# Last stage of a two-block network on one core: its output products in two groups of four token tiles instead of 4 + 2 + 2, and another order of banks, buffers and steps where the stage begins

## The chip, the cores and the metric

One core of a Trainium2 chip runs the whole program. The metric is device time in microseconds (us), median of the runs shown. Engines are named as the profile names them: PE (TensorE matmuls), PEld (its weight loads), DVE (VectorE), ACT (ScalarE), POOL (GpSimd), SP (SyncE, which issues nearly all DMAs here; "SPq" is its queue).

## The reference, cut to what matters

A first block (gated delta rule, gated linear attention, convolutional FFN) and a second block (dilated windows, a bidirectional recurrence, cross attention) come before the part that changes. Everything is fp32, 1024 tokens, width 1024. The part that changes is the end of the second block:

```python
h = h + memory_cross_attention(h, mem)  # ends in o @ wo         ("w_co")
hid = square(relu(rmsnorm(h, norm_mlp_g) @ w_mlp_in))       # 1024 -> 4096  ("mlp_in")
h = h + hid @ w_mlp_out                                     # 4096 -> 1024  ("mlp_out")
return rmsnorm(h, norm_final_g)                             # ("norm_final")
```

## The kernel before, in words

**Order.** `schedule` (line 351) writes one list of units. Each engine's program runs through the whole list in that order and does its own share of each unit, so an engine's queue is in order: a wait of one unit holds all that is behind it. SP is such a queue too: it carries panel loads (line 3519), stores of hidden tiles (line 3694), the spill of the residual (line 3682) and the final stores (line 3709).

**Products.** An fp32 factor is split into a high and a low word (fp32r), and a product is three matmuls of 128x512 (`wide`, line 1366). A panel is 512 KB of weights (or of hidden values), [128, 1024] in SBUF. SP loads it, ACT writes its high word (`halve`, line 2778), then POOL (line 3280) or, for panels in `on_dve`, DVE (line 1837) writes the low word over the panel itself. SP loads ahead through a ring of 6 panel slots (10 in the output products); high words sit in a ring of 9. ACT works up to 5 split panels ahead of the unit that uses one, DVE up to 3 of its own, POOL up to 2 of its own. A slot or a high place is free again once PE has done with the last unit that used it.

**Head of the MLP.** `grouped_products` (line 202) does w_co for token tiles (0-3), (4,5), (6,7). Between its units stand the RMS norm of the finished tiles (ACT squares, line 2879; DVE Newton steps, lines 1948 to 1954; ACT xhat, line 2888) and transposes into features: PE line 1363 into a bank, two ACT writes (2864 feat_x, 2865 ftm_hi), one DVE write (2045 ftm_lo) that frees the bank. Steps f1, f2, f3 are the features of the tiles (0-3), (4,5), (6,7); each is 8 chunks of 128 features.

The hidden layer has 16 pairs m of chunks of 128 features, by two halves l of 512 tokens. Pair 0 is computed plainly: `whole(i, l)` is chunk i, half l, 24 matmuls. Pairs 1 to 15 use a seven-product (Winograd) form, `mlp_pair(m)`, products P1, P2, P5, P6, P7, P3, P4 of 12 matmuls each. That form needs sums of weight panels (POOL line 3476, S1 to S4, their high words by ACT line 3215, their low words by POOL line 3454) and sums T1 to T4 of the features (`feature_sums`: DVE lines 2660 to 2663, high words ACT line 3235, low words DVE line 2666). The order at the head (lines 794 to 804) is: `in_split_rest(0)`, which writes `in_first` and `in_b`, the high words of pair 0's second panel (ACT lines 3205, 3206); `whole(0,0)` and `whole(1,0)` in banks 4 and 5; f3, in banks 2, 3, 6, 7, 0, 1 in turn; `in_split(1)`, which writes the sums and words of pair 1's weights; `feature_sums`; `whole(0,1)` and `whole(1,1)` in banks 2 and 3; `in_split_sums(1)`, the words of the weight sums.

ACT copies each whole result out of its bank (`mlp_in`, line 3220) and DVE squares it (line 2670) at the place of its `whole` unit. `in_first` lies in a buffer that w_co uses till its end, so ACT waits there for the last product of w_co (line 3203).

**Output products.** `mlp_out` (line 1799) goes over the groups (0-3), (4,5), (6,7) of tiles (`GROUPS`, line 198). In a group it goes over k0, 16 steps of two chunks each, and in a step over the two halves h of the output width. It holds 8, 4 and 4 banks (`out_banks`, line 832). Each step needs two weight panels, and a panel of hidden values, which for the first group holds two chunks and for the others four; so a group takes 48, 40 and 40 panels, and a step is 48 matmuls in the first group and 24 in the others. When a group ends, DVE adds its banks to the residual (line 2720), then come squares, Newton steps, and further on the `final` steps: DVE line 2071 scales tile n, SP stores it (line 3709) after a wait for that. Tiles 0 to 3 have their `final` at the steps k0 = 14, 16, 18, 20 of the second group, tiles 4 and 5 at k0 = 14 and 16 of the third, tiles 6 and 7 at the end.

Of the kernel before, what the change touches and what calls it, by code (L numbers as in the profile page):

```python
# [350 lines left out]
def schedule(k):  # L351
# [417 lines left out]
    f3, a3 = feats("norm_mlp", (6, 7), (2, 3, 6, 7, 0, 1)), applies("norm_mlp", (6, 7))  # L769
# [32 lines left out]
    for i in range(2):  # L802
        whole(i, 1)
    k.unit("in_split_sums", 1)
    outs = []
    for m in range(1, NPAIRS):
# [19 lines left out]
        for what in PRODUCTS:  # L826
            k.banks.take(("mlp_in", m, what), (4, 5, 6, 7, 0, 1, 2, 3))
# [4 lines left out]
    out_banks = ((5, 6, 7, 0, 1, 2, 3, 4), (5, 6, 7, 0), (1, 2, 3, 4))  # L832

    def final(n):
        return lambda: k.unit("final", n, 0)

    between = {(0, 8): [lambda: k.unit("resid_again")],
               (0, NFF2 - 2): [lambda: norm_start(k, "norm_final", (0, 1, 2, 3))],
               (1, NFF2 - 2): [lambda: norm_start(k, "norm_final", (4, 5))],
               (2, NFF2 - 2): [lambda: norm_start(k, "norm_final", (6, 7)), final(6), final(7)],  # L840
               **{(1, 14 + 2 * n): [final(n)] for n in range(4)}, **{(2, 6 + 2 * n): [final(n)] for n in (4, 5)}}
    for group, tiles, k0, ph, pw in outs:
        for h in range(HALVES):
            if k0 == 0:
                for n in tiles:
                    k.banks.take(("mlp_out", h, n), out_banks[group])
            k.unit("mlp_out", h, k0, tiles, pw[h], ph, used=pw[h],
                   last=("mlp_out", h, tiles[-1]) if k0 == NFF2 - 2 else None)
# [38 lines left out]
def memory(k, nc, stack):  # L887
# [187 lines left out]
    k.in_first = place("in_first", [P, BANK], F32R, at=at(10))  # L1075
# [2689 lines left out]
```

## Time and profile before

| what | value |
|---|---|
| median of 3 runs (lowest, highest) | 2972.49 us (2966.23, 2973.3) |
| the profiled execution's own time | 2970.01 us |
| its span | 2968.8 us, so 1.2 us lie around the span |
| matmul busy share of the span | 95% |
| w_co | from 2207.9 us |
| pair 0 and the features of tiles 6, 7 | 2262.9 to 2302.1 us |
| output products | 2591.5 to 2959.2 us |

The profiled execution lies 2.5 us under the median. A row of a timeline or of the chain of waits gives start, duration, engine, line and operation; in square brackets is the idle time of the engine ahead of it and what ended that. Durations of matmuls overlap, so the pace is read from one start to the next. In a table of stretches the columns are start:end, length, then for each engine the busy time and (xcount) of instructions, then the granted TensorE clock (1.00 is 2.4 GHz, 0.50 is 1.2 GHz), the DMA share and GB/s.

### The profile page before, as it was taken

To read this page: it belongs to the slowest core of one execution; us is meant where nothing else is said; L and a number is where in the kernel's file an instruction comes from. 1 tells how busy PE (TensorE), PEld (TensorE's weight loads), DVE (VectorE), ACT (ScalarE), POOL (GpSimd) and SP (SyncE) were. 2 spreads that over 40 slices of the span, in tenths; PEclk is the share of its full clock that TensorE was granted. 3 is DMA by queue.
4 is the path that set the end of the run, shared out by engine and by line. 5 is a ranking of instruction groups with operands and counts; after the bars stand their busy time and mean duration, and the time that the engine had idled before them with its cause. 6 is when DMAs were issued, how large, how long until landed. Compare 5 with 4: busy or idle time off the path is not lost.

```text
span 2968.8 us, 33195 instructions
## 1 busy us (share of the span) xinstructions
PE 2821.9 (95%) x13188; PEld 2199.7 (74%) x13188; DVE 1658.4 (56%) x2418; ACT 1032.1 (35%) x1577; POOL 989.5 (33%) x565
## 2 busy tenths in 40 slices
PE   6999999999999999999998999999988999999988
PEld 3777567776467888888886678887756888888876
DVE  7556655543874554556556656776345644533454
ACT  2346522223022222222225640674456322132443
POOL 2432012222144444444440214210012877522343
PEclk9999999999999999999999999999998999999999
DMA  7210022214332111111113122113212333364565
GB/s 257 88 41 22 5 82 72 65 57 143 125 94 72 49 50 50 50 49 44 50 43 125 39 57 81 34 42 107 66 42 92 110 110 112 111 227 147 201 235 181
DMA packets 241306, 269.11 MB, mean 91 GB/s; under 512 B 18792, under 2 KB 158464, under 8 KB 241152
## 3 DMA queue, kind: packets, MB, share of 16 engines
q1 hardware_dynamic: 239520, 262.59, 26.9%
q10 hardware_dynamic: 1631, 4.40, 0.4%
q8 instruction: 105, 1.72, 0.2%
q14 instruction: 50, 0.40, 0.0%
HBM read 229.96 MB, written 34.87 MB: 89 GB/s over the span
## 4 chain that ended last, share of the span: by engine, by line
PE 75%; DVE 11%; ACT 6%; DMA 3%; issue 3%; POOL 2%; SPq 0%; ACTq 0%; DVEq 0%; POOLq 0%
PE bank L1370 60%; PE bank L1716 2%; DMA panel<-in_w_mlp_out 2%; PE bank L1518 1%; PE bank L1477 1%; PE bank L1532 1%; PE bank L1700 1%; PE bank L1668 1%; DVE ffn_conv L2403 1%; PE bank L1483 1%; PE bank L1363 1%; DVE ffn_conv L2399 1%; PE bank L1687 1%; DVE mixed L2109 1%; DVE panel_lo L1837 1%
## 5 line engine op out<-in xcount | busy, mean ns | idle before, releaser
L1370 PE MATMUL bank<-ft_hi,panel_lo 128*128 128x512 f32 x1312 | 467.6, 391 | 1.7 <-DVE ftx_lo L2045 1.7
L1370 PEld LDWEIGHTS bank<-ft_hi,panel_lo 128*128 128x128 f32 x1312 | 247.2, 188 | 54.1 <-issue 2.8
L1370 PE MATMUL bank<-ft_hi,panel_hi 128*128 128x512 f32 x704 | 273.9, 389 | 0.0
L1370 PE MATMUL bank<-ft_lo,panel_hi 128*128 128x512 f32 x704 | 273.9, 389 | 0.0
L2399 DVE TENSOR_SCALAR ffn_conv<-ffn_in,ffn_taps 128x512 f32<-128x512 f32 x88 | 114.1, 1297 | 278.8 <-ACT ffn_in L3065 278.6
L3280 POOL TENSOR_TENSOR panel_lo<-panel,panel_hi 128x1024 fp32r<-128x1024 f32 x66 | 158.0, 2401 | 244.3 <-ACT panel_hi L2778 231.1
L1370 PE MATMUL bank<-panelm_hi,panelm_hi 128*128 128x512 f32 x512 | 201.3, 393 | 14.2 <-POOL panel_out_lo L3280 8.6
L1370 PE MATMUL bank<-ft,panel 128*128 128x512 f32 x416 | 202.5, 607 | 2.3 <-ACT sq_inv L3018 0.9
L2403 DVE SCALAR_TENSOR_TENSOR ffn_conv<-ffn_in,ffn_taps,ffn_conv 128x512 f32<-128x512 f32 x176 | 154.5, 878 | 6.2
L1837 DVE TENSOR_TENSOR panel_lo<-panel,panelm_hi 128x1024 fp32r<-128x1024 f32 x52 | 83.5, 1611 | 125.7 <-ACT panelm_hi L2778 125.7
L1370 PEld LDWEIGHTS bank<-ft_hi,panel_hi 128*128 128x128 f32 x704 | 132.1, 188 | 27.5
L1370 PEld LDWEIGHTS bank<-ft_lo,panel_hi 128*128 128x128 f32 x704 | 132.1, 188 | 27.4
L3374 POOL TENSOR_TENSOR ltm_vnew<-lt,masks 128x512 f32<-128x512 f32 x48 | 65.0, 1362 | 249.4 <-PE bank L1518 145.7
L1370 PE MATMUL bank<-panel_hi,ffn_hid_hi 128*128 128x512 f32 x352 | 138.4, 393 | 5.1 <-ACT ffn_in L3065 4.2
L2682 DVE TENSOR_TENSOR mlp_y<-mlp_y,bank 128x512 f32<-128x512 f32 x105 | 72.1, 686 | 125.6 <-ACT mlp_y L3228 74.7
L1370 PE MATMUL bank<-panel_hi,ffn_hid_lo 128*128 128x512 f32 x352 | 138.1, 392 | 0.0
L1370 PE MATMUL bank<-panel_lo,ffn_hid_hi 128*128 128x512 f32 x352 | 138.1, 392 | 0.0
L2778 ACT ACTIVATE panelm_hi<-panel 128x1024 fp32r<-128x1024 f32 x78 | 82.4, 1060 | 148.6 <-DMA panel<-in_w_mlp_out 75.9
L2414 DVE TENSOR_TENSOR resid<-resid,bank 128x512 f32<-128x512 f32 x176 | 111.7, 683 | 35.4 <-PE bank L1370 35.1
L1370 PE MATMUL bank<-panel_lo,panelm_hi 128*128 128x512 f32 x320 | 124.5, 389 | 0.0
L1370 PEld LDWEIGHTS bank<-panelm_hi,panelm_hi 128*128 128x128 f32 x512 | 96.9, 189 | 37.1 <-POOL panel_out_lo L3280 9.4
L2778 ACT ACTIVATE panel_hi<-panel 128x1024 fp32r<-128x1024 f32 x66 | 69.4, 1054 | 140.6 <-PE bank L1370 102.9
(544 smaller groups left out, 6832.4 us busy)
## 6 DMA issues: line engine op xcount, KB each, us to landing
panel<-in_w_mlp_out SPq DMA_DIRECT2D x60, 512.0 KB, 6.7
panel<-in_w_in SPq DMA_DIRECT2D x52, 512.0 KB, 3.8
panel<-in_w_ada SPq DMA_DIRECT2D x48, 512.0 KB, 4.1
panel<-in_ffn_w_up SPq DMA_DIRECT2D x44, 512.0 KB, 3.7
panel_out<-in_w_mlp_out SPq DMA_DIRECT2D x36, 512.0 KB, 6.1
panel<-in_w_mlp_in SPq DMA_DIRECT2D x32, 512.0 KB, 5.1
hid<-mlp_y SPq DMA_DIRECT2D x60, 256.0 KB, 2.0
panel<-in_w_o SPq DMA_DIRECT2D x24, 512.0 KB, 3.5
```

What stands on the lines that cost most here:

```text
L1363: m = te.transpose(ps[:, tile(i)], src[:, tile(j)], k.ident[:])
L1370: m = te.matmul(ps, a, b, start=(start and j == 0), stop=(stop and j == len(pairs) - 1))
L1477: m = te.matmul(ps[:, tile(h)], lhs(h), rhs_of(h), start=True, stop=True)
L1716: m = te.matmul(ps[:, at:at + HD + 1], k.p_t[(2 * t + hb) % 4][:, 2 * side + c, :], v, start=(hb == side == c == 0), stop=(hb == side == c ...
L1837: dve.tensor_tensor(lo, k.view(p), hi.bitcast(F32), ALU.subtract).then_inc(*v.new("lowered", p))
L2399: dve.tensor_scalar(out, pre[:, 1 + h * BANK:1 + (h + 1) * BANK], w[:, 0:1], w[:, 3:4], ALU.mult, ALU.add).then_inc(*v.new("ffn_tap", c, g ...
L2403: dve.scalar_tensor_tensor(out, pre[:, 1 + j + h * BANK:1 + j + (h + 1) * BANK], w[:, j:j + 1], out, ALU.mult, ALU.add).then_inc(*v.new("f ...
L2414: evict(dve.tensor_tensor(r, r, v.bank("down", i, h, n)[:], ALU.add), "down", i, h, n)
L2682: return dve.tensor_tensor(out[:], x[:], v.bank("mlp_in", m, what)[:], ALU.add)
L2778: act.activation(k.halves_of(p)[0], k.view(p), ACT.Copy).then_inc(*a.new("halved_hi", p))
L3280: pool.tensor_tensor(lo, k.view(p), hi.bitcast(F32), ALU.subtract).then_inc(*g.new("halved_lo", p))
L3374: pool.tensor_tensor(t.ltm[:], t.lt[:], spread(k.masks[:, lv, :], 1, H4), ALU.mult).then_inc(*g.new("delta_pool", n, "ltm", lv))
```

## The change

1. **Output products**: groups (0-3), (4-7). Every step has a hidden panel of two chunks and two weight panels: 48 + 48 panels. Both groups hold all eight banks, in the order 5, 0, 1, 2, 3, 6, 7, 4.
2. **Between them**: squares of tiles 0 to 3 at k0 = 2, 4, 6, 8 of the second group, Newton steps at 10, finals at 12, 14, 16, 18.
3. **Last chunks**: the steps k0 = 28 and 30 of the second group are done by pairs of tiles: `mlp_last` for (4,5), h = 0 and 1, then norm and finals of 4 and 5; then the same for (6,7).
4. **Head, order**: all of `in_split(0)` stands where its first half stood (after w_co's unit (1,3)). `in_first` has another place, so ACT doesn't wait there for w_co. Both buffer sets of `in_s`, `sums` and `sums_lo` change places between odd and even pairs, so POOL's sums of pair 1 wait for the last w_co product only, no longer for the features and squares of tiles 6 and 7.
5. **Head, banks**: `whole(0,0)`, `whole(1,0)` in banks 6, 7; f3 over banks 0 to 5; the ring of the seven products begins 4, 5, 0, 1, 2, 3, 6, 7.
6. **Feature sums in two halves** of the token columns: those of tiles (0,1) with (4,5) ahead of f3, the rest behind it. High and low words as before, after the second half.
7. **`squared_whole`**: the four copies, squares and stores of pair 0 come together after the last `whole`.

```diff
-    f3, a3 = feats("norm_mlp", (6, 7), (2, 3, 6, 7, 0, 1)), applies("norm_mlp", (6, 7))
+    f3, a3 = feats("norm_mlp", (6, 7), (0, 1, 2, 3, 4, 5)), applies("norm_mlp", (6, 7))
     def whole(i, l):
-        k.banks.take(("mlp_in", 0, i, l), (((4, 5), (2, 3))[l][i],))
+        k.banks.take(("mlp_in", 0, i, l), (((6, 7), (2, 3))[l][i],))
-    k.unit("in_split_rest", 0)
+    in_panels(1)
     for i in range(2):
         whole(i, 0)
+    k.unit("feature_sums", 0)
     for step in f3:
         step()
-    in_panels(1)
     k.unit("in_split", 1)
-    k.unit("feature_sums")
+    k.unit("feature_sums", 1)
     for i in range(2):
         whole(i, 1)
+    k.unit("squared_whole")
     k.unit("in_split_sums", 1)
...
-            for group, tiles in enumerate(GROUPS):
+            for group, tiles in enumerate(((0, 1, 2, 3), (4, 5, 6, 7))):
                 for k0 in range(0, NFF2, 2):
-                    if group == 0 or k0 % 4 == 0:
-                        chunks = 4 if group else 2
-                        ph = k.panel("mlp_hid", (group, k0),
-                                     rows_of(d["hid"], k0 * P, chunks * P, tiles[0] * P, len(tiles) * P), True)
-                        k.hid_key[ph] = min(group, 1), k0 // 2, chunks // 2
+                    ph = k.panel("mlp_hid", (group, k0), rows_of(d["hid"], k0 * P, 2 * P, group * BANK, BANK), True)
+                    k.hid_key[ph] = k0 // 2, group
...
-    out_banks = ((5, 6, 7, 0, 1, 2, 3, 4), (5, 6, 7, 0), (1, 2, 3, 4))
+    out_banks = (5, 0, 1, 2, 3, 6, 7, 4)
     between = {(0, 8): [lambda: k.unit("resid_again")],
-               (0, NFF2 - 2): [lambda: norm_start(k, "norm_final", (0, 1, 2, 3))],
-               (1, NFF2 - 2): [lambda: norm_start(k, "norm_final", (4, 5))],
-               (2, NFF2 - 2): [lambda: norm_start(k, "norm_final", (6, 7)), final(6), final(7)],
-               **{(1, 14 + 2 * n): [final(n)] for n in range(4)}, **{(2, 6 + 2 * n): [final(n)] for n in (4, 5)}}
+               (1, 10): [lambda: k.unit("deviation", "norm_final", 0, 4)],
+               **{(1, 2 + 2 * n): [lambda n=n: k.unit("squares", "norm_final", n)] for n in range(4)},
+               **{(1, 12 + 2 * n): [lambda n=n: k.unit("final", n, 0)] for n in range(4)}}
...
+            if group == 0 or k0 < NFF2 - 4:
+                k.unit("mlp_out", h, k0, tiles, pw[h], ph, used=pw[h],
+                       last=("mlp_out", h, tiles[-1]) if k0 == NFF2 - 2 else None)
...
+    for tiles in ((4, 5), (6, 7)):
+        for h in range(HALVES):
+            k.unit("mlp_last", h, tiles, outs[-2:], used=outs[-1][4][1])
+        norm_start(k, "norm_final", tiles)
+        for n in tiles:
+            k.unit("final", n, 0)
...
-    k.in_first = place("in_first", [P, BANK], F32R, at=at(10))
+    k.in_first = place("in_first", [P, BANK], F32R, at=at(29, 256))
-    k.mlp_first = [place(f"mlp_first{n}", [P, BANK], at=at(8, 2048 * n)) for n in range(4)]
+    k.mlp_first = [place(f"mlp_first{n}", [P, BANK], at=at(26, 2304 + 2048 * n)) for n in range(4)]
...
+    def mlp_last(h, tiles, outs):
+        for n in tiles:
+            ps = pe.bank("mlp_out", h, n)
+            for _, _, k0, ph, pw in outs:
+                w, x = panel(pw[h]), panel(ph)
+                for j in range(2):
+                    m = wide(ps[:], [y[:, j, tile(n - 4)] for y in x], [y[:, j, :] for y in w], False, k0 + j == NFF2 - 1)
+            fill(m, "mlp_out", h, n)
...
-    def feature_sums():
+    def feature_sums(part):
+        cols = slice(2 * P * part, 2 * P * part + 2 * P)
+        (x0, z0), (x1, z1) = ((k.feat_x[l][:, 0:4, cols], k.feat_x[l][:, 4:KD, cols]) for l in range(2))
+        v.wait_ge("ft_hi", "norm_mlp", 4 + 2 * part, KD - 1)
...
     def in_split(m):
             if m == 1:
-                g.wait_ge(*g.filled("feat", "norm_mlp", 6, KD - 1))
-                g.wait_ge("squares", "norm_mlp", NT - 1)
+                for n in (6, 7):
+                    g.wait_ge(*g.filled("w_co", 1, n))
```

## Rows read from the trace of the kernel before

**Rows 1.** The page, busy time of each engine with share and count.

```profile
PE 2821.9 (95%) x13188; PEld 2199.7 (74%) x13188; DVE 1658.4 (56%) x2418; ACT 1032.1 (35%) x1577; POOL 989.5 (33%) x565
```

**Rows 2.** Stretches: head of the MLP; first group of output products; second and third.

```profile
2262.00:2310.00 48.00, 37.35 (x138) 29.30 (x139) 29.13 (x31) 26.40 (x41) 20.63 (x10) 0.82 0.13 44
...
2604.00:2762.00 158.00, 157.82 (x696) 130.70 (x697) 54.28 (x33) 49.05 (x47) 39.29 (x17) 1.00 0.49 179
...
2780.00:2867.00 87.00, 79.10 (x339) 64.31 (x338) 45.84 (x30) 37.37 (x37) 36.82 (x14) 0.98 0.68 235
2867.00:2959.00 92.00, 87.80 (x380) 71.69 (x378) 42.56 (x39) 39.45 (x39) 35.24 (x14) 0.98 0.61 211
```

**Rows 3.** Timeline of PE at the head: last transposes of f2 up to P5.

```profile
2259.41 1.03 PE L1363 MATMUL bank<-ident,xhat 128*128 128x128 f32 x8
...
2262.85 0.67 PE L1370 MATMUL bank<-ftm_hi,in_a 128*128 128x512 f32 x1 [2.41 <-DVE ftm_lo L2045]
...
2273.85 0.79 PE L1370 MATMUL bank<-ftm_hi,in_first 128*128 128x512 f32 x1 [3.67 <-POOL panel_lo L3454]
...
2282.32 1.47 PE L1363 MATMUL bank<-ident,xhat 128*128 128x128 f32 x12
...
2288.87 0.80 PE L1370 MATMUL bank<-ftm_hi,in_a 128*128 128x512 f32 x1 [3.20 <-DVE ftm_lo L2045]
...
2309.64 0.47 PE L1370 MATMUL bank<-feat_x_hi,in_s 128*128 128x512 f32 x1 [1.92 <-POOL sums_lo L3454]
```

**Rows 4.** Timeline of PE in the output products, the first and the longest of seven gaps.

```profile
2604.18 0.50 PE L1370 MATMUL bank<-panelm_hi,panelm_hi 128*128 128x512 f32 x1 [1.61 <-POOL panel_lo L3280]
...
2839.55 0.60 PE L1370 MATMUL bank<-panelm_hi,panelm_hi 128*128 128x512 f32 x1 [5.01 <-POOL panel_out_lo L3280]
```

**Rows 5.** Timeline of SP's queue: a load, and the next final store.

```profile
2829.91 0.78 SPq L3519 DMA_DIRECT2D panel_out<-in_w_mlp_out  x1
...
2843.91 0.36 SPq L3709 DMA_DIRECT2D out<-resid  x1
```

**Rows 6.** Chain of waits, from a panel's load to its low word.

```profile
2844.86 6.25 DMA panel<-in_w_mlp_out
2851.14 1.07 ACT panelm_hi L2778
2852.27 2.36 POOL panel_lo L3280
```

**Rows 7.** Timeline of ACT at the head.

```profile
2267.56 2.19 ACT L2888 ACTIVATE xhat<-resid,rstd 128x1024 f32<-128x1024 f32 x2 [2.41 <-DVE rstd L1954]
...
2270.17 0.61 ACT L3206 ACTIVATE in_b<-panel 128x512 fp32r<-128x512 f32 x1
...
2283.00 0.48 ACT L2864 ACTIVATE feat_x<-bank,cols 128x256 f32<-128x256 f32 x1
...
2288.36 0.59 ACT L2865 ACTIVATE ftm_hi<-bank,cols 128x256 fp32r<-128x256 f32 x1
...
2299.47 5.53 ACT L3235 ACTIVATE feat_x_hi<-feat_x 128x2048 fp32r<-128x2048 f32 x3 [5.70 <-DVE feat_x L2662]
2304.90 1.06 ACT L3220 COPY mlp_first<-bank 128x512 f32<-128x512 f32 x2
2305.83 2.03 ACT L3215 ACTIVATE in_s<-sums 128x1024 fp32r<-128x1024 f32 x2
```

**Rows 8.** Timeline of DVE at the head: feature sums and their low words.

```profile
2289.46 2.28 DVE L2660 TENSOR_TENSOR feat_x<-feat_x,feat_x 128x2048 f32<-128x2048 f32 x1
...
2295.06 4.37 DVE L2662 TENSOR_TENSOR feat_x<-feat_x,feat_x 128x2048 f32<-128x2048 f32 x1
...
2302.78 13.24 DVE L2666 TENSOR_TENSOR feat_x_lo<-feat_x,feat_x_hi 128x2048 fp32r<-128x2048 f32 x4
```

**Rows 9.** Timeline of POOL at the head.

```profile
2306.99 6.87 POOL L3454 TENSOR_TENSOR sums_lo<-sums,in_s 128x1024 fp32r<-128x1024 f32 x2 [6.40 <-ACT in_s L3215]
```

**Rows 10.** Timeline of DVE after the last matmul.

```profile
2959.22 0.69 DVE L2720 TENSOR_TENSOR resid<-resid,bank 128x512 f32<-128x512 f32 x1 [0.67 <-PE bank L1370]
```

More of the change, by code:

```diff
@@ L826, in schedule @@
         for what in PRODUCTS:
-            k.banks.take(("mlp_in", m, what), (4, 5, 6, 7, 0, 1, 2, 3))
+            k.banks.take(("mlp_in", m, what), (4, 5, 0, 1, 2, 3, 6, 7))
         pa, pb = k.in_panels[m]
@@ L845, in schedule @@
                 for n in tiles:
-                    k.banks.take(("mlp_out", h, n), out_banks[group])
-            k.unit("mlp_out", h, k0, tiles, pw[h], ph, used=pw[h],
-                   last=("mlp_out", h, tiles[-1]) if k0 == NFF2 - 2 else None)
+                    k.banks.take(("mlp_out", h, n), out_banks)
+            if group == 0 or k0 < NFF2 - 4:
+                k.unit("mlp_out", h, k0, tiles, pw[h], ph, used=pw[h],
+                       last=("mlp_out", h, tiles[-1]) if k0 == NFF2 - 2 else None)
         k.hid_with[ph], k.last_use[ph] = pw[1], len(k.order) - 1
@@ L2713, in mlp_out, with mlp_last, sums_out @@
     def mlp_out(h, k0, tiles, pw, ph):
-        if k0 != NFF2 - 2:
-            return
+        if k0 == NFF2 - 2:
+            sums_out(h, tiles)
+    def mlp_last(h, tiles, outs):
+        sums_out(h, tiles)
+    def sums_out(h, tiles):
         v.wait_ge("resid_loaded", "again")
@@ L2751, in halve @@
         elif k.panel_list[p][0] in ("mlp_hid", "mlp_out"):
[L2752 removed]
+            a.wait_ge(*a.filled("mlp_in", NPAIRS - (2 if k.high_at[p] in [f"True {n}" for n in range(4)] else 1), "P4"))
         if k.panel_list[p][3] is not None:
@@ L3202, in in_split_rest @@
         if m == 0:
-            for n in (6, 7):
-                a.wait_ge(*a.filled("w_co", 1, n))
             act.activation(k.in_first[:], b[:, 0:BANK], ACT.Copy)
@@ L3208, in in_split_sums @@
     def in_split_sums(m):
-        s = m % 2
-        if m == 2:
+        s = 1 - m % 2
+        if m == 1:
+            for n in (6, 7):
+                a.wait_ge(*a.filled("w_co", 1, n))
+        elif m == 2:
             for n in range(4):
@@ L3216, in in_split_sums, with squared_whole @@
                 *a.new("halved_hi", "S", m, 12 + 22 * n))
-    def mlp_in(i, l):
-        a.wait_ge(*a.filled("mlp_in", 0, i, l))
-        evict(act.copy(k.mlp_first[2 * i + l][:], a.bank("mlp_in", 0, i, l)[:]), "mlp_in", 0, i, l)
+    def squared_whole():
+        for l in range(2):
+            for i in range(2):
+                a.wait_ge(*a.filled("mlp_in", 0, i, l))
+                evict(act.copy(k.mlp_first[2 * i + l][:], a.bank("mlp_in", 0, i, l)[:]), "mlp_in", 0, i, l)
     def mlp_pair(m):
@@ L3228, in mlp_pair, with feature_sums @@
         evict(act.copy(k.mlp_y[n][:], a.bank("mlp_in", m, "P1")[:]), "mlp_in", m, "P1")
-    def feature_sums():
+    def feature_sums(part):
+        if part == 0:
+            return
         a.wait_ge("resid_moved0", "mlp", 0)
@@ L3469, in in_split @@
                 g.wait_ge("panel_loaded%d" % k.slot[p], p)
-            x = [k.sums[s][n // 2][:, n % 2, :] for n in range(4)]
+            x = [k.sums[1 - s][n // 2][:, n % 2, :] for n in range(4)]
             for n, (u, w, op) in enumerate(((b[:, 0:BANK], b[:, BANK:D], ALU.add), (x[0], a[:, 0:BANK], ALU.subtract),
@@ L3513, in load @@
         if p in k.hid_key:
-            l, first, count = k.hid_key[p]
-            for m in range(first, first + count):
-                for i in range(2):
-                    sp.wait_ge("moved%d" % (4 * (m % 2) + 2 * i + l), "hid", m)
+            m, l = k.hid_key[p]
+            for i in range(2):
+                sp.wait_ge("moved%d" % (4 * (m % 2) + 2 * i + l), "hid", m)
         name = "panel_loaded%d" % k.slot[p]
@@ L3694, in store, with squared_whole @@
         sync.dma_start(d["hid"][tile(2 * m + i), half(l)], y[:]).then_inc(*sp.new("moved%d" % n, "hid", m, step=16))
-    def mlp_in(i, l):
-        sp.wait_ge("mlp_square", 0, i, l)
-        store(0, i, l, k.mlp_first[2 * i + l])
+    def squared_whole():
+        for l in range(2):
+            for i in range(2):
+                sp.wait_ge("mlp_square", 0, i, l)
+                store(0, i, l, k.mlp_first[2 * i + l])
     def mlp_pair(m):
```

58 lines of the change are left out of this document (27 added, 31 removed).

## Prediction, written before the change was run

> **What bounds the kernel now.** I read the page first: PE is busy for 95% of the span [rows 1], so only its gaps and its slow stretches can be won. The change adds and removes no matmul. Then the table of stretches, and in the stretches that lose time the timeline of PE with the idle time ahead of each matmul.
>
> The pace to compare with comes from the first group of output products: 696 matmuls in 158 us, 0.227 us each, no gap [rows 2]. So 24 matmuls (a `whole`, or half a step) take 5.45 us, a step of 48 takes 10.9, and one of the seven products takes 2.7. Two places fall short of it.
>
> *Head of the MLP.* From 2262 to 2310 the granted clock averages 0.82 [rows 2]. As the clock has two levels, 1.2 and 2.4 GHz, (1 - 0.82) x 48 = 8.6 us of full-speed work are lost. The gaps are 2.41, 3.67, 3.20 and 1.92 us [rows 3], and the timeline shows the matmuls right behind them at half pace. Each has its own releaser: a bank that a feature write had not freed, the low word of pair 0's second panel, the features of tiles 6 and 7, the low word of the weight sums.
>
> *Second and third group of output products.* 339 matmuls take 87 us where 77.0 would do, and 380 take 92 where 86.3 would do [rows 2]: 10.0 + 5.7 = 15.7 us lost. The longest gap, 5.01 us, ends with POOL's low word of a panel [rows 4]. What made it late stands in SP's queue: load at 2829.91, next final store only at 2843.91 [rows 5]. SP waits for `final`, DVE's `final` stands behind a low word, that behind a load: 14 us a round, against 5.45 us that PE needs for a step of two tiles.
>
> **The change, part by part** (against the profiled execution, 2970.0 us, span 2968.8).
>
> *1. Start of `whole(0,0)`.* Banks 6 and 7 were freed long before (w_co, h = 0), so the wait for a feature write goes. The transposes ended at 2259.41 + 1.03 = 2260.4 [rows 3]. But ACT now writes `in_first` and `in_b`, 0.61 us each [rows 7], ahead of the last features of f1 and f2, and PE's transposes follow ACT there: between 0 and 1.2 us later, and I take 1.0 as ACT has little idle time there. Start 2261.4 instead of 2262.85: gain 1.4.
>
> *2. The two wholes.* The low words of pair 0 are now ready about 2256, as POOL has only their ACT words to wait for, so the 3.67 us gap goes, and with both gaps the slow matmuls. They took 2262.85 to 2282.32, 19.5 us [rows 3]; 48 x 0.227 = 10.9: gain 8.6. Call their end t0: 2272.3 instead of 2282.3. POOL's sums of pair 1 move to 2261, where nothing needs it. xhat of tiles 6, 7 began at 2267.56 and took 2.19 [rows 7]; one microsecond later it still ends (2270.8) before t0.
>
> *3. f3 and `whole(0,1)`.* Before: 6.55 us from t0 to 2288.87 [rows 3]. Now no copy stands ahead of the features on ACT. ACT writes sixteen pieces from 2283.00 to 2288.95 [rows 7], 0.72 us a chunk with its start to start; DVE adds half a microsecond (2288.95 to 2289.46 [rows 7, 8]). The half sums put ahead on DVE are four operations of half of 2.28 us [rows 8], with overhead 1.2 each: from 2268.5 (after the Newton steps) to 2273.4, t0 + 1.1, so they hold the bank writes hardly at all. Chunks 6 and 7 wait for banks 0 and 1, `whole(0,1)` for bank 2 (chunk 2): 0.3 + 3 x 0.72 + 0.5 = 3.0, start at t0 + 3.2. Its last features are there at t0 + 6.6, wanted at 8.0. Gain 3.3.
>
> *4. Up to P5 of pair 1.* PE would come to P5 at t0 + 3.2 + 10.9 + 5.45 = 19.6. What it needs: DVE's second half sums start at t0 + 6.7. Four operations of half length: 2.28 us alone, 4.37 beside POOL for a whole one [rows 8], so 4 x 1.2 = 4.8 to 4 x 2.2 = 8.8; POOL has but two instructions to collide there, so I take 6.6. The third is done at 11.7, then ACT's three high words 5.53, four copies 2.1 (1.06 for two), one weight word 1.0 [rows 7], POOL's low word 2.7 (start 2306.99, PE 2309.64 [rows 9, 3]): 23.1. The four copies, which had been spread, now stand two more in this chain. So PE waits 3.5 us, more than before, yet P5 is at t0 + 23.1 instead of 27.3. Beyond point 3 that is 0.9 of gain; the longer wait costs clock, 0.5, so 0.4. The low words on DVE (13.24 for four [rows 8]) end at t0 + 26.5, before P4 at 34, and the squares behind them end before the stores are wanted. The pairs after that run as now.
>
> The Trainium skill (SBUF - State Buffer, Who interferes with whom) says that a DVE operation with two SBUF inputs and a GpSimd one that reads SBUF lock each other out for the whole instruction. The two durations of the sums agree. Taken for all four sums it would make the 6.6 a full 8.8 and take 2.2 us from the gain.
>
> *5. Start and change of group.* The 1.61 us gap behind the first step [rows 4] stays: the fifth panel still waits for the last pair. At the change of group DVE adds the four banks of h = 0 (0.69 each [rows 10]) while PE does h = 1, and the squares that stood there are spread behind. No cost, one part of a microsecond of gain that I don't count.
>
> *6. Second group.* A step has 10.9 us for three panels, as the first group had, which ran without gap. Loads per 48 matmuls fall from five to three. SP's finals at k0 = 12 to 18: a round of 14 us against 10.9, four times, is 12 us of lag at most, and ten slots are 3.3 steps, 36 us. So 15.7 us come back.
>
> *7. Last pairs of tiles.* `mlp_last` needs the panels of k0 = 30 only 1.4 us after step 26. The latest, the first weight panel, can be loaded when step 24 ends: 6.25 + 1.07 + 2.36 + 0.4 to issue = 10.1 us [rows 6], against 10.9 + 1.4 = 12.3. Bound: with a load of twice that length it would be 4 us late. Norm and finals of tiles 4, 5 run under the last 10.9 us of PE.
>
> *8. Tail.* From the last bank add at 2959.22 [rows 10] to the end, 9.6 us, the steps are the same: 0.
>
> Sum: 1.4 + 8.6 + 3.3 + 0.4 + 15.7 = 29.4 us. The execution becomes 2940.6; it lay 2.5 below the median, so the median is forecast at **2943**. Bounds: the head between 8 (point 4 with 8.8, dips behind the bank waits of f3, more delay in point 1) and 18 (no wait at P5), the output between 10 and 17. Both ends give 2937 to 2954.
>
> **The rivals.**
>
> *A. The head gives back half.* ACT carries the chain of point 4 in order, and PE, early, waits at P5. If copies, sums and lock each come late, P5 stays at t0 + 27.3 as it was and the longer gap (7.7 us) costs 2 us of clock. For it: this wait exists already (1.92 us). Against: half the sums are out of the chain. 29.4 - 4 - 2 = 23: 2949.
>
> *B. Banks.* Both groups hold all eight banks. If DVE's adds queue behind a low word whose panel is late, the second group can't begin: 8 x 0.69 = 5.5 us: 2948. Against: the first change of group in the trace shows only a small gap. The Trainium skill (Perfetto Trace Analysis, Matmuls) asks that groups rotate through different banks, so that one is emptied under the next; by it this wait would come here.
>
> *C. The finals still empty the ring.* If SP's rounds are not covered by the ten slots, 4 x (14 - 10.9) = 12.4 us of gap return: 2955.
>
> *D. The change doesn't do what it says:* the gaps only move, to other panels and other words; gain under 9: about 2970.
>
> *E. Slower.* In the second group every step from k0 = 2 to 26 loses what the longest gap shows, 5.0 us, since hidden panel, weights, squares and finals share SP's and DVE's queues: 13 x 5.0 = 65, so 2972 - 14 - 16 + 65 = 3007. It decides when a round takes longer than the 36 us of the ring; the longest round seen is 14.
>
> **How the numbers follow.** Forecast 0.66, A 0.12, B 0.06, C 0.08, D 0.05, E 0.03. A measurement of this kernel tells about 0.3% (9 us) from no change. Faster by more: forecast, A, B, C, 0.92; within: D, 0.05; slower: E, 0.03. The range runs from 2936 to 2954: the forecast's bounds, A and B.
>
> **What would show it.** In the changed kernel's timeline of PE: no gap before `whole(0,0)` and `whole(1,0)`; they take about 11 us together; short gaps in f3; a gap of 3 to 4 us before P5 ended by `sums_lo`; P1 of the last pair some 14 us earlier. In the output products the gap behind the first step and no other over 1 us, clock 1.00, SP's final stores without long waits. Wrong would be: `whole(0,0)` waiting for POOL, P5 over 25 us behind t0, gaps ended by `panel_lo` in the second group or at `mlp_last`, or a longer tail.

## The result, and the profile after

The changed kernel took 2943.66 us (median of 4 executions, 2942.52 to 2945.87) where the kernel before took 2969.36 (median of 4, 2965.34 to 2973.3) on the same chip: ratio 0.9914, 95% interval 0.9897 to 0.9932. On a second chip, beside the experiments below, it was 2938.75 against 2970.38: ratio 0.9894, 0.9881 to 0.9908. The forecast was 2943, with a range of 2936 to 2954. The profiled execution took 2943.77 us (span 2942.5), 26.3 us less than the profiled one of before.

Two executions of one kernel can't be laid on each other by their absolute times: they differ by some microseconds ahead of the part that was changed. The last common point is the first `w_co` product. This is it in the timeline of PE, in the kernel before, with the wait ahead of the last features of the first group:

```profile
2207.92 0.47 PE L1370 MATMUL bank<-panel_co,mix_co_hi 128*128 128x512 f32 x1 [1.57 <-DVE mix_co_lo L2648]
...
2250.60 0.66 PE L1363 MATMUL bank<-ident,xhat 128*128 128x128 f32 x4 [1.19 <-DVE ftm_lo L2045]
```

And this is the timeline of PE after, from the same point to P5 of pair 1 (the first product that needs the weight sums), with its first gap in the output products:

```profile
2208.63 0.47 PE L1371 MATMUL bank<-panel_co,mix_co_hi 128*128 128x512 f32 x1 [1.57 <-DVE mix_co_lo L2657]
...
2252.13 0.66 PE L1364 MATMUL bank<-ident,xhat 128*128 128x128 f32 x4 [2.06 <-DVE ftm_lo L2054]
...
2254.39 0.63 PE L1371 MATMUL bank<-panel_co,mix_co_lo 128*128 128x512 f32 x1
...
2262.52 0.47 PE L1371 MATMUL bank<-ftm_hi,in_a 128*128 128x512 f32 x1
...
2273.50 0.49 PE L1364 MATMUL bank<-ident,xhat 128*128 128x128 f32 x3
...
2276.86 0.50 PE L1371 MATMUL bank<-ftm_hi,in_a 128*128 128x512 f32 x1 [0.28 <-DVE ftm_lo L2054]
...
2299.70 0.77 PE L1371 MATMUL bank<-feat_x_hi,in_s 128*128 128x512 f32 x1 [6.21 <-POOL sums_lo L3472]
...
2595.39 0.50 PE L1371 MATMUL bank<-panelm_hi,panelm_hi 128*128 128x512 f32 x1 [1.81 <-POOL panel_lo L3298]
```

Against [rows 3] the 2.41 and 3.67 us gaps are gone and the two wholes run through in 10.98 us. The 3.20 is 0.28. But the wait for the low word of the weight sums has grown from 1.92 to 6.21, and a gap of 2.06 us stands ahead of the last features of the first group, where the kernel before has 1.19.

The stretches of the output products (window, its length, PE's busy time and matmuls, granted clock, DMA share, GB/s), against [rows 2]:

```profile
2595.00:2753.00 158.00, 157.61 (x695) 1.00 0.49 179
...
2771.00:2858.00 87.00, 87.00 (x385) 1.00 0.47 163
2858.00:2932.00 74.00, 74.00 (x328) 1.00 0.33 121
```

The second group now has 385 matmuls in 87 us where 339 stood, with no gap; so has the stretch of the change of group and of the last pairs of tiles.

From the first product of `w_co` to the end the times are 2968.8 - 2207.92 = 760.9 and 2942.5 - 2208.63 = 733.9 us: **27.0 us** gained, and 0.7 of it hidden by a later start in this execution. A second profiled execution of the changed kernel gives 733.9 again, though its absolute times lie 0.6 us lower. All single runs below are compared by this time. It doesn't repeat that well for every kernel: the kernel of before with only its last steps changed reaches P5 1.5 us earlier than the kernel before (see its run below), since fewer matmuls run slowly in its head. So a difference of 1 to 2 us between single profiles counts only where a timeline shows what made it. In parts, from the rows of before and of after:

| stretch | before | after | gain | forecast |
|---|---|---|---|---|
| first `w_co` to `whole(0,0)` | 54.9 | 53.9 | 1.0 | 1.4 |
| the two wholes | 19.5 | 11.0 | 8.5 | 8.6 |
| f3 to `whole(0,1)` | 6.55 | 3.36 | 3.2 | 3.3 |
| to P5 of pair 1 | 20.8 | 22.8 | -2.1 | 0.9 |
| P5 to the last bank add | 649.6 | 633.3 | 16.3 | 15.7 less 0.5 |
| tail | 9.6 | 9.5 | 0.1 | 0 |

The last bank add of after is this one, of DVE:

```profile
2933.00 0.69 DVE L2737 TENSOR_TENSOR resid<-resid,bank 128x512 f32<-128x512 f32 x1 [2.03 <-PE bank L1371]
```

What makes P5 late stands in three timelines of the changed kernel. DVE, from the second half sums on:

```profile
2280.38 1.22 DVE L2669 TENSOR_TENSOR feat_x<-feat_x,feat_x 128x1024 f32<-128x1024 f32 x1
2281.62 3.31 DVE L2670 TENSOR_TENSOR feat_x<-feat_x 128x1024 f32<-128x1024 f32 x1
2284.97 2.20 DVE L2671 TENSOR_TENSOR feat_x<-feat_x,feat_x 128x1024 f32<-128x1024 f32 x1
2287.20 1.22 DVE L2672 TENSOR_TENSOR feat_x<-feat_x,feat_x 128x1024 f32<-128x1024 f32 x1
2288.46 8.90 DVE L2676 TENSOR_TENSOR feat_x_lo<-feat_x,feat_x_hi 128x2048 fp32r<-128x2048 f32 x4
2297.27 8.98 DVE L2680 SCALAR_TENSOR_TENSOR mlp_first<-mlp_first 128x512 f32<-128x512 f32 x4
```

ACT, which waits for the third of them:

```profile
2287.20 5.53 ACT L3253 ACTIVATE feat_x_hi<-feat_x 128x2048 fp32r<-128x2048 f32 x3 [3.58 <-DVE feat_x L2671]
2292.63 2.03 ACT L3236 COPY mlp_first<-bank 128x512 f32<-128x512 f32 x4
2294.53 2.04 ACT L3229 ACTIVATE in_s<-sums 128x1024 fp32r<-128x1024 f32 x2
```

And POOL:

```profile
2280.96 2.88 POOL L3472 TENSOR_TENSOR panel_lo<-panel,in_a 128x1024 fp32r<-128x1024 f32 x1 [13.78 <-ACT in_a L3212]
2283.82 2.27 POOL L3472 TENSOR_TENSOR panel_lo<-panel,in_b 128x512 fp32r<-128x512 f32 x1
2295.69 6.64 POOL L3472 TENSOR_TENSOR sums_lo<-sums,in_s 128x1024 fp32r<-128x1024 f32 x2 [9.61 <-ACT in_s L3229]
```

The reader's first question to such a chain: which of its members had been ready before? The weight sums were, since about 2267 (POOL's four sums start at 2262.02). Their words stand last on ACT only because the order puts them there.

### The profile page after: what moved, and what is told of

Its sections match the earlier page's. It is cut to its first block, busy times and chain, and to the rows that moved or that the text cites. A ratio compares the mean times of both kernels' runs of the same rounds, so it can differ in the third digit from the quotient of the medians.

```text
span 2942.5 us, 33094 instructions
## 1 busy us (share of the span) xinstructions
PE 2810.1 (95%) x13188; PEld 2191.6 (74%) x13188; DVE 1618.1 (55%) x2406; ACT 998.0 (34%) x1545; POOL 938.9 (32%) x549
## 4 chain that ended last, share of the span: by engine, by line
PE 78%; DVE 10%; ACT 6%; issue 2%; POOL 2%; DMA 2%; SPq 0%; ACTq 0%; DVEq 0%; POOLq 0%
PE bank L1371 63%; PE bank L1717 2%; PE bank L1519 1%; PE bank L1478 1%; PE bank L1533 1%; PE bank L1701 1%; PE bank L1669 1%; DVE ffn_conv L2412 1%; PE bank L1484 1%; DVE ffn_conv L2408 1%; PE bank L1364 1%; PE bank L1688 1%; DVE mixed L2118 1%; POOL panel_lo L3298 1%; PE bank L1736 1%
## 5 line engine op out<-in xcount | busy, mean ns | idle before, releaser
L3392 POOL TENSOR_TENSOR ltm_vnew<-lt,masks 128x512 f32<-128x512 f32 x48 | 64.9, 1362 | 246.5 <-PE bank L1519 142.8
L1846 DVE TENSOR_TENSOR panel_lo<-panel,panelm_hi 128x1024 fp32r<-128x1024 f32 x40 | 62.5, 1567 | 126.4 <-ACT panelm_hi L2796 126.4
L1371 PE MATMUL bank<-panelm_hi,panel_lo 128*128 128x512 f32 x320 | 124.5, 389 | 0.0
L2796 ACT ACTIVATE panelm_hi<-panel 128x1024 fp32r<-128x1024 f32 x60 | 63.5, 1060 | 169.6 <-PE bank L1371 88.9
```

The lines of the kernel that those rows point to most:

```text
L1371: m = te.matmul(ps, a, b, start=(start and j == 0), stop=(stop and j == len(pairs) - 1))
L1846: dve.tensor_tensor(lo, k.view(p), hi.bitcast(F32), ALU.subtract).then_inc(*v.new("lowered", p))
L2796: act.activation(k.halves_of(p)[0], k.view(p), ACT.Copy).then_inc(*a.new("halved_hi", p))
L3392: pool.tensor_tensor(t.ltm[:], t.lt[:], spread(k.masks[:, lv, :], 1, H4), ALU.mult).then_inc(*g.new("delta_pool", n, "ltm", lv))
```

## The experiments

### The two halves alone, and the change again

The first has the hunks of the output products only (groups, `between`, `mlp_last`, the hidden panels), the second all others. Their banks are renamed to fit.

> Kernel before with the output part of the change alone (two groups of four tiles, squares and finals spread, last chunks by pairs of tiles); its head is that of before. Theory (the two parts are independent): head as before, P5 of pair 1 near 2309.6; from then to the end as in the changed kernel, so output stage about 350 us instead of 367.7, no gap over 2 us in it; gain 16 to 18 us, about 2953. Rival (the output part needs the buffers or banks of the new head): gaps ended by panel words or by feature banks at the start or at the change of group, gain under 13.

> Changed kernel with the output part of before (groups of 4, 2 and 2 tiles). Theory: P5 of pair 1 near 2299.7 as in the changed kernel, everything behind it about 10 us earlier than before and as long as before; gain 9 to 11 us, about 2960; the output stage keeps its gap of 5 us and its 16 us of loss. Rival (an earlier output stage only waits longer for its panels): gain under 6.

> The changed kernel itself, on the same chip as its two halves. If the parts are independent, its gain is the sum of the gains of the two halves within 1 us (about 17 + 10 = 27); if they help or hinder each other, it is off the sum by over 2 us.

On one chip (five executions of each half, four of the whole): output only 2950.32 us, ratio 0.9927 (0.9914 to 0.9939); head only 2960.62, 0.9969 (0.9956 to 0.9981); both 2938.75, 0.9894. From the first `w_co` product: 743.4, 752.7 and 733.9, so 17.5, 8.2 and 27.0 us gained. The halves sum to 25.6, 1.4 short of the whole, between the two expectations. The head alone lies under its forecast of 9 to 11: it brings P5 10.6 us forward, but then takes 652.1 us to the last bank add where the kernel before takes 649.6. Of these 2.5, 1.1 are the slow matmuls behind the longer wait at P5, which the whole change has too. The other 1.4 are what the halves lack to the whole: the head-only kernel keeps the seven gaps of before in its output products, 14.6 us in all against 14.2 (the longest are 5.10, 2.50 and 3.80 us), and twenty matmuls run slowly behind them instead of fifteen. With the output part alone there is none behind the one of 1.67 us at the start. About two thirds of the gain (17.5 of 25.6) is the output's.

### What freed the output products: the finals

In the kernel before, the finals of tiles 0 to 5 go behind the last product:

```diff
-               (2, NFF2 - 2): [lambda: norm_start(k, "norm_final", (6, 7)), final(6), final(7)],
-               **{(1, 14 + 2 * n): [final(n)] for n in range(4)}, **{(2, 6 + 2 * n): [final(n)] for n in (4, 5)}}
+               (2, NFF2 - 2): [lambda: norm_start(k, "norm_final", (6, 7)), *(final(n) for n in range(8))]}
```

> Kernel before, with the finals of tiles 0 to 5 moved behind the last product, to those of tiles 6 and 7; nothing of them is left between the loads. Theory (finals in SP's and DVE's queues empty the ring of panels): the gaps of 5.0, 2.4 and 3.6 us go, the second and third group lose under 3 us of the 15.7, and the tail grows from 9.6 to about 17 to 25 us. Rival (the rate of panels, five for 48 matmuls against three, is too much for loads and low words): gaps of over 2 us stay in both groups, 8 us or more lost.

Its stretches in the second and third group, of two tiles each:

```profile
2778.00:2865.00 87.00, 86.66 (x383) 1.00 0.70 242
2865.00:2938.00 73.00, 73.00 (x322) 1.00 0.63 216
```

The long gaps are gone, two of 0.46 and 0.34 us are left: 383 matmuls in 87 us, at 242 GB/s. So the old groups ask for no more panels than the queues can bring. From P5 (2308.26 here) to the last bank add it takes 633.2 us, against 649.6 before and 633.3 after. The whole gain of the output part on PE is that finals no longer stand between the loads of steps of 5.45 us. A final is both a scaling on DVE and a store in SP's queue; no run parts the two. The tail is 17.6 us instead of 9.6, as expected. That leaves 8.3 of the 16.4; the kernel gains 9.9 in all (751.0), and the other 1.5 are not of this edit: its head is that of before, with the same waits of 3.67 and 3.20 us, but six and seven matmuls run slowly behind them, where the kernel before has fourteen and eleven, and P5 is reached at 100.2 instead of 101.7. What the groups of four bring is steps of 10.9 us under which the finals cost nothing.

In the changed kernel the four finals stand together:

```diff
-               **{(1, 12 + 2 * n): [lambda n=n: k.unit("final", n, 0)] for n in range(4)}}
+               (1, 12): [lambda n=n: k.unit("final", n, 0) for n in range(4)]}
```

> Changed kernel, with the four finals of tiles 0 to 3 (DVE's scaling and the store in SP's queue) all behind step 12 of the second group, not one every second step. Theory (SP's rounds run 14 us each in the kernel before because each final stands between two loads; together they cost SP one round of at most 14 + 3 x 3 = 23 us, and the ten panel slots hold 36): no gap of PE over 0.5 us, 733.9 us from the first w_co product as before. Rival (finals must be spread, or loads come late): a gap of 1 us or more, ended by a panel's word, within 30 us behind the finals.

No gap behind the one at the start (1.70), 733.6 us; SP issues the four stores within 7.0 us. Four finals in a row are no burden; a final between every two loads of a short step was.

### The last products by pairs of tiles

```diff
-            if group == 0 or k0 < NFF2 - 4:
+            if True:
...
-    for tiles in ((4, 5), (6, 7)):
-        for h in range(HALVES):
-            k.unit("mlp_last", h, tiles, outs[-2:], used=outs[-1][4][1])
+    for tiles in ((4, 5, 6, 7),):
```

> Changed kernel, without the last products by pairs of tiles: the last two steps of the second group go over its four tiles like the others, then norm and finals of all four. Theory (two more tiles of squares and finals stand in the tail, 1.3 to 2.6 us each): the tail from the last bank add to the end grows from 9.5 to 12.5 to 15.5 us, the end 3 to 6 us later. Rival (stores overlap, the order of the last steps is worth nothing): under 1 us.

The tail is 12.3 us (last bank add at 2929.40, span 2941.7), and the whole 736.4: 2.5 later. `mlp_last` is worth that; a little under what was expected. The timeline of DVE shows what the two more tiles add: four finals in place of two.

```profile
2933.75 4.87 DVE L2078 SCALAR_TENSOR_TENSOR resid<-resid,rstd,norm_rows 128x1024 f32<-128x1024 f32 x4
```

### P5: the lock, the halves, the order

POOL's low word of pair 1's second panel goes behind those of the weight sums (the last hunk stands at the end of `in_split_sums`):

```diff
-        if m:
+        if m > 1:
             less(k.low[pb][:, BANK:D], b[:, BANK:D], k.in_b[s][:], "B", m)
-        else:
+        elif m == 0:
...
+        if m == 1:
+            pb = k.slot[k.in_panels[1][1]]
+            less(k.low[pb][:, BANK:D], k.panels[pb][:, BANK:D], k.in_b[1][:], "B", 1)
```

> Changed kernel, with POOL's low word of pair 1's second panel (wanted only at P4) moved from ahead of the low words of the weight sums to behind them; POOL is then idle beside the third of DVE's second half sums. Times count from the first w_co product. Theory (each of DVE's sums that meets a POOL instruction takes 2.2 to 3.3 us instead of 1.2, and the chain over ACT to P5 follows): the third sum takes 1.2 instead of 2.2 us, the second the same 3.3; ACT's three high words, the copies, the weight word and P5 come 1.0 us earlier (P5 at 90.1 instead of 91.1), the end 0.5 to 1.0 us. Rival (the long sums are DVE's own, or POOL's last word alone sets P5): the third sum stays at 2.2, P5 where it was, 733.9.

DVE's same four sums, and PE's P5:

```profile
2277.04 1.22 DVE L2669 TENSOR_TENSOR feat_x<-feat_x,feat_x 128x1024 f32<-128x1024 f32 x1
2278.29 3.31 DVE L2670 TENSOR_TENSOR feat_x<-feat_x 128x1024 f32<-128x1024 f32 x1
2281.64 1.22 DVE L2671 TENSOR_TENSOR feat_x<-feat_x,feat_x 128x1024 f32<-128x1024 f32 x1
2282.90 1.22 DVE L2672 TENSOR_TENSOR feat_x<-feat_x,feat_x 128x1024 f32<-128x1024 f32 x1
```

```profile
2295.40 0.76 PE L1371 MATMUL bank<-feat_x_hi,in_s 128*128 128x512 f32 x1 [5.21 <-POOL sums_lo L3472]
```

The third sum fell from 2.20 to 1.22 us, and P5 came at 2295.40 - 2205.25 = 90.15, 0.9 earlier: the theory, to a tenth. The end gained 2.1, twice what was expected (731.8). The other 1.2 are the clock: behind the shorter wait half as many matmuls run slowly, six starts 0.43 us or more apart, against twelve in the changed kernel; the granted clock over 15 us from just ahead of P5 is 0.89 here and 0.81 there. That the shorter wait is the reason isn't shown by one profile: five profiles with the wait of 6.2 us have twelve, twelve, twelve, twelve and eleven slow matmuls behind it, but behind the wait of 3.67 us of the kernel before two profiles have fourteen and a third has six.

The feature sums in one piece, as before:

```diff
-        cols = slice(2 * P * part, 2 * P * part + 2 * P)
+        if part == 0:
+            return
+        cols = slice(0, BANK)
...
-        v.wait_ge("ft_hi", "norm_mlp", 4 + 2 * part, KD - 1)
+        v.wait_ge("ft_hi", "norm_mlp", 6, KD - 1)
```

> Changed kernel, with the feature sums in one piece behind the features of tiles 6 and 7, as before, not in halves. Theory (halves take one half of DVE's sums out of the chain to P5): DVE's sums take 4 to 6 us longer behind the features, P5 of pair 1 comes 4 to 5 us later than its 26.2 us behind the two whole products, less about 0.5 as the features are held no more, and the end is 3.5 to 5 us later. Rival (POOL's words and ACT's copies set P5, not the sums): P5 and the end move by under 1.5 us.

P5 at 93.2, the end at 736.1: 2.1 and 2.3 later, between theory and rival. DVE's timeline says why 4 to 5 was too much:

```profile
2280.54 2.28 DVE L2671 TENSOR_TENSOR feat_x<-feat_x,feat_x 128x2048 f32<-128x2048 f32 x1
2282.86 4.38 DVE L2672 TENSOR_TENSOR feat_x<-feat_x 128x2048 f32<-128x2048 f32 x1
2287.28 3.26 DVE L2673 TENSOR_TENSOR feat_x<-feat_x,feat_x 128x2048 f32<-128x2048 f32 x1
2290.57 2.29 DVE L2674 TENSOR_TENSOR feat_x<-feat_x,feat_x 128x2048 f32<-128x2048 f32 x1
```

Whole or half, a meeting with POOL adds the same: 4.38 - 2.28 and 3.31 - 1.22 are both 2.1 (beside POOL's word of 1024), 3.26 - 2.28 and 2.20 - 1.22 both 1.0 (beside the one of 512). So halving saves 3 x 1.05 = 3.2 us up to the end of the third sum, for which ACT waits, and no part of the meetings. Of the 3.2 P5 lost only 2.1, since POOL's first low word, begun later, took less.

ACT's and POOL's words of the weight sums ahead of the second half of the feature sums:

```diff
     k.unit("in_split", 1)
+    k.unit("in_split_sums", 1)
     k.unit("feature_sums", 1)
...
     k.unit("squared_whole")
-    k.unit("in_split_sums", 1)
```

> Changed kernel, with ACT's and POOL's words of the weight sums of pair 1 issued ahead of the second half of the feature sums (ACT had idled 3.6 us there; the weight sums are ready from about 2265). Theory (order on ACT makes P5 late: high words of features, four copies, then the weight words): low word of the sums starts near 2286 instead of 2295.7, P5's wait of 6.2 us falls under 1 us (DVE's first low word of the features, due about 2290.7, is earlier than PE's 2293.3) and with it the slow matmuls behind it; gain over the changed kernel 5 to 7 us, about 2937.5. Rival (the lock: POOL's low words now run beside DVE's sums and low words and both stretch): P5 still waits 3 us or more, ended by POOL or by DVE's low word, gain under 3 us.

P5 came at 86.4 instead of 91.1, behind a wait of 1.51 us, but the end did not move (734.4; the median of four is 2940.44 against 2938.75 for the changed kernel on the same chip). The 5 to 7 us that were expected did not come. This is PE, P5 and a wait behind P4, in the next pair:

```profile
2289.14 0.50 PE L1371 MATMUL bank<-feat_x_hi,in_s 128*128 128x512 f32 x1 [1.51 <-DVE feat_x_lo L2676]
...
2310.72 0.80 PE L1371 MATMUL bank<-ftm_hi,in_a 128*128 128x512 f32 x1 [3.79 <-ACT mlp_y L3244]
```

And these are DVE, ACT and SP there:

```profile
2284.70 14.27 DVE L2676 TENSOR_TENSOR feat_x_lo<-feat_x,feat_x_hi 128x2048 fp32r<-128x2048 f32 x4
2298.90 6.88 DVE L2680 SCALAR_TENSOR_TENSOR mlp_first<-mlp_first 128x512 f32<-128x512 f32 x4
```

```profile
2308.19 2.00 ACT L3229 ACTIVATE in_s<-sums 128x1024 fp32r<-128x1024 f32 x2 [17.91 <-DMA hid<-mlp_first]
2310.10 0.57 ACT L3244 COPY mlp_y<-bank 128x512 f32<-128x512 f32 x1
```

```profile
2300.70 5.42 SPq L3712 DMA_DIRECT2D hid<-mlp_first  x4
```

The weight words of pair 2 go where the four whole results lie, so ACT stands 17.9 us until they are stored, and the copy that frees PE's bank stands behind it. The changed kernel has this chain too, but there it is early enough and another wait ends last:

```profile
2308.66 2.01 ACT L3229 ACTIVATE in_s<-sums 128x1024 fp32r<-128x1024 f32 x2 [10.64 <-POOL sums L3495]
```

Counted from the first `w_co` product ACT writes these words at 100.0 us in the changed kernel and at 105.4 with early words, 5.4 later, and PE now comes to the bank some 6 us earlier. The 5.4 us come from DVE: POOL, released early, works beside DVE's low words all along (its words of the weight sums, then the sums of pair 2), and they take 14.27 us instead of 8.90, so the squares end at 103.0 instead of 97.6 and the stores follow. So the rival had the lock right, and the place wrong: it cost little at P5 and all of the gain behind it. At 100.0 the words would have been no hindrance: in the changed kernel the copy behind them is done at 102.5, and PE, with early words, comes to the bank at 104.2.

### Room for the next pair, and the two together

On top of the early words, the four results move to the buffers of the pair products, which are free at this time and whose reuse already waits for the stores:

```diff
-    k.mlp_first = [place(f"mlp_first{n}", [P, BANK], at=at(26, 2304 + 2048 * n)) for n in range(4)]
+    k.mlp_first = k.mlp_y[0:4]
...
-        elif m == 2:
-            for n in range(4):
-                a.wait_ge("moved%d" % n, "hid", 0)
...
     def squared_whole():
+        a.wait_ge(*a.filled("mlp_in", 0, 1, 1))
```

> The kernel with the words of the weight sums issued early, and with the four results of the whole products kept in the buffers of the pair products (free at this time) instead of where the next pair's weight words go. In the run with early words P5 came 4.7 us earlier and a wait of 3.8 us stood behind it: ACT waited for the stores of the four results before it wrote the next weight words, and its copy of P1 stood behind them. Theory (that buffer alone held it): no wait over 1 us from P5 on, and the 4 to 5 us reach the end: from the first w_co product to the end 729 to 730.5 us instead of 733.9. Rival (DVE's 14.3 us of low words and 6.9 of squares, or POOL's sums of the next pair, are late just as well): another wait of 2 to 4 us, ended by DVE or POOL, and 733 to 734.5.

729.3 us from the first `w_co` product, 4.5 less than the changed kernel; four executions have the median 2935.39, ratio 0.9889 (0.9870 to 0.9908). DVE's low words take as long as with early words (14.29 us), but ACT's copy for the bank no longer waits for the stores behind them. The 3.79 us wait is gone; PE keeps one of 1.54 at P5 and one of 1.25, ended by DVE, where none over 1 was expected:

```profile
2317.07 0.50 PE L1371 MATMUL bank<-feat_x_hi,in_s 128*128 128x512 f32 x1 [1.25 <-DVE mlp_y L2694]
```

By the time from the first `w_co` product it is the fastest kernel here. By the medians (2935.39 here, 2938.75 for the changed kernel) the difference lies inside the intervals.

### The words of pair 0's second panel

They go behind the features of tiles 4 and 5 (ACT's words of the second panel become a unit of their own), in the changed kernel and in the fastest one, that of the last section:

```diff
-        (2, 3): [f2[2], f2[3], lambda: norm_start(k, "norm_mlp", (6, 7)), *a3, away((6, 7))]},
+        (2, 3): [f2[2], f2[3], lambda: k.unit("in_split_rest", 0), lambda: norm_start(k, "norm_mlp", (6, 7)), *a3, away((6, 7))]},
...
```

> Changed kernel, with ACT's words of the second panel of pair 0 (and POOL's low words of them) moved from ahead of the last features of tiles 0 to 3 to behind the features of tiles 4 and 5. Executions drift by some us before the part looked at, so times are counted from the first w_co product. Theory (these two words, 1.2 us, delayed the transposes and so let the clock fall for nine w_co products): PE's gap of 2.06 us there goes back to 1.19, the products behind it keep the full pace, the first whole product starts 2 to 3 us earlier than its 53.9 us after the first w_co product, and 1 to 2.5 us of it reach the end (733.9 us falls to 731.5 to 733), since DVE's half sums, which come when they came, then hold the features of tiles 6 and 7. Rival: the clock falls all the same, or the second panel's low word comes too late for the second whole product (a gap ended by POOL); no gain.

> Early words, the other buffer, and the words of pair 0's second panel behind the features of tiles 4 and 5, together. Theory (the three are independent waits): the sum of the two gains, 5.5 to 7.5 us less than the changed kernel from the first w_co product to the end (726.5 to 728.5), about 2934. Rival (one chain on ACT takes the place of the other): no better than the better of the two alone.

The gap is 1.19 us again, none of the `w_co` products behind it is slow, and `whole(0,0)` starts at 52.3 instead of 53.9. But the end is later: 735.3 (1.4 more than the changed kernel) and 731.5 (2.1 more than the fastest one); four executions of the latter have the median 2938.43. So the two moves don't add, as the rival of the second run had it. This is PE with the words moved in the changed kernel:

```profile
2266.46 0.50 PE L1371 MATMUL bank<-ftm_hi,in_first 128*128 128x512 f32 x1 [0.67 <-POOL panel_lo L3477]
...
2274.04 0.30 PE L1364 MATMUL bank<-ident,xhat 128*128 128x128 f32 x1 [1.84 <-ACT xhat L2906]
2274.99 2.61 PE L1364 MATMUL bank<-ident,xhat 128*128 128x128 f32 x11 [0.65 <-ACT xhat L2906]
```

The words now stand ahead of the norm of tiles 6 and 7. Its xhat begins 64.9 us after the first `w_co` product instead of 61.3, and PE waits for it. The 0.67 us gap ended by POOL is the one that the rival named; the later xhat neither theory named. `whole(0,1)` starts at 71.3 instead of 68.2, and P5 comes 2.4 us (93.5) and 2.9 us (89.3 against 86.4) later than without the move. The place in the change is the better one.

## Why the prediction was right, and which steps were off

*Point 1.* The transposes were 1.2 us later at most by the forecast; the gap there grew by 0.87, in the range. What the point left out is the clock: behind the 2.06 us gap eight `w_co` products run at half pace (2254.39 above is one, 0.63 us each), from 2253.98 on. Start of `whole(0,0)` 1.0 earlier, not 1.4. With the words moved away it came 1.6 earlier still, which sizes gap and clock together.

*Points 2 and 3.* As forecast: 10.98 for 10.9, 3.36 for 3.2. The half sums on DVE ended at t0 + 1.4 (t0 is the end of the two wholes, 2273.50 here), with the features hardly held.

*Point 4* is the step that failed, in two sizes. It put P5 at t0 + 23.1 behind a wait of 3.5 us; it came at t0 + 26.2 (2273.50 to 2299.70) behind one of 6.21. By the forecast's own signs that is wrong: they name "P5 over 25 us behind t0". P1 of the last pair was to come some 14 us earlier; the output products behind it start 9.5 earlier: their first gap is 386.8 us behind the first `w_co` product, against 396.3 before. The mechanism was the one named: the wait grows, ended by `sums_lo`, on a chain from DVE's sums over ACT's words and copies to POOL. ACT's part was right (8.5 us for 8.6). **The sums** were taken at 6.6 us, 1.65 each, and took 8.0, and the third, for which ACT waits, was done at t0 + 13.7, not 11.7. The bound of 8.8 scaled a half sum by the ratio of a whole one; the runs show an addition for each POOL instruction instead, 2.1 and 1.0 us: 4 x 1.22 + 3.1 = 8.0. The trace of before had them: beside the 2.28 and the 4.37 of [rows 8] stand the other two of the four whole sums, 3.26 and 3.27 us, so 0, 1.0, 2.1 and 1.0 more than the 2.28 of one alone:

```profile
2291.77 3.26 DVE L2661 TENSOR_TENSOR feat_x<-feat_x 128x2048 f32<-128x2048 f32 x1
...
2299.47 3.27 DVE L2663 TENSOR_TENSOR feat_x<-feat_x,feat_x 128x2048 f32<-128x2048 f32 x1
```

**POOL's low word** was taken at 2.7 and took 4.0 (2295.69 to 2299.70), since DVE was still at the low words of the features when it began. And the dip behind a 6.2 us wait has twelve slow matmuls, 2.5 us, against seven before and two partly slow; 0.5 more was forecast and 0.9 came.

The Trainium skill (SBUF - State Buffer, Who interferes with whom) calls this an exclusive lock held for the whole instruction. By that rule, the trace agrees: POOL's words end at 2283.84 and 2286.09, and DVE's second and third sum 1.1 us behind each, about the 1.22 of one alone; and what DVE loses follows the length of POOL's instruction and not that of its own. The forecast priced it at 8.8, above the middle it took; the measured 8.0 is nearer to it.

*Points 5 to 8.* The gap behind the first step stayed (1.81). The 15.7 us came back, and the run with the finals moved shows that it was the finals, as [rows 5] said, and not the number of panels: the step "loads per 48 matmuls fall from five to three" carried next to nothing (0.8 us of gaps were left with the old groups). SP's four stores in the second group are issued 10.9 us apart (2827.75, 2838.62, 2849.50, 2860.39), one a step, without long waits. `mlp_last` was in time, no gap there. The tail kept its length, which the forecast booked as 0; without `mlp_last` it would have been 2.8 longer.

*The rivals.* A is what happened in part: P5 at t0 + 26.2, between 23.1 and 27.3, and the longer gap cost clock; its 2949 was too late as P5 did not fall all the way back and the output gave what it should. B did not come: both groups hold all eight banks and the 18 us around the change of group run without a gap (81 matmuls, clock 1.00), since DVE adds the banks of h = 0 under the products of h = 1. The Trainium skill (Perfetto Trace Analysis, Matmuls) asks for a rotation through banks so that one group is emptied under the next; here the rotation is inside the group, and that suffices. C, D and E did not come.

Behind the median (2943.66 for 2943) stands luck. Aligned, the gain was 27.0 and not 29.4: 3.0 lost at P5, 0.6 in points 1 to 3, 1.2 more than forecast from P5 to the end, tail included. The first chip's medians differ by 25.7, 3.7 under the forecast; the forecast counted from 2972.49, and the kernel before gave 2969.36 beside the changed one, 3.1 less, and the two errors nearly cancel. The second chip's medians differ by 31.6.

## What to carry to other kernels

Before a store or a scaling is put between loads in one queue, compare its round with the time of a step: six finals cost 16 us in steps of 5.45 us, four of them cost nothing in steps of 10.9. When an operation is late because of its place in an engine's order, ask which members of the chain are ready long before and put those first; then look what waits behind, since a P5 that came 4.7 us earlier reached the end only after the next buffer had been freed as well; and look what the earlier work now runs beside, since POOL's held DVE's low words up by 5.4 us. And align two traces at the last common instruction before small differences are read, then count the slow matmuls in both: they alone made 1.5 us between two profiles whose heads are the same code.

## What the runs showed that was not expected

- Executions of one kernel differ before the changed part: the first `w_co` product lies between 2200.27 and 2210.33 us over the fourteen profiles here, while the time from there to the end is 733.9 twice for the changed kernel. The kernel of before needs 101.7 us from there to P5 in two profiles (the second with the new output part) and 100.2 in a third (finals at the end), with the same code up to there: behind the same wait of 3.67 us eight fewer matmuls run slowly in the third, and its two wholes take 17.9 us instead of 19.5.
- DVE and POOL hold each other up by whole instructions in both directions: DVE's four low words of features take 8.90 us with POOL idle for most of them, 11.06 with the sums in one piece, and 14.27 where POOL works beside them all along (early words), against 13.24 before [rows 8]. POOL's first low word of the weight sums takes 4.0 where it begins beside them; its words of the same size take 2.4 to 2.6 us in the later pairs.
- How many matmuls run slowly behind a wait is not in proportion to it, and not the same from one profile to the next: twelve (once eleven) behind 6.2 us, six behind 5.21, none behind 1.51, seven behind 1.92 before, six to eight behind the 2.06 us gap in nine profiles, and fourteen or six behind 3.67. The runs don't tell why.
